# Gated linear attention: half of a head's first joint projection moved ahead of its first turn of keys, and low weight chunks moved ahead of the last chunk's gating

## The reference, cut to what matters

```python
q_g, k_g, v_g, r_g, gk_f, gk_b = ...              # columns of h @ w_in
lg_f = log_sigmoid(gk_f @ w_gk2_f + b_gk_f) / 16  # and lg_b
b = cumsum(logg, axis=3)                          # within a chunk
qe, ke, kd = q * exp(b), k * exp(-b), k * exp(b_last - b)
A = tril(qe @ ke.T);  o_intra = A @ v
kv_chunk = kd.T @ v
S_next = exp(b_last) * S + kv_chunk               # scan over chunks
o = o_intra + qe @ S
o_g = rms_norm(o_f + flip(o_b), g_gla) * silu(r_g)
```

## Time and profile before

| | us |
|---|---|
| median of 3 runs | 2572.76 |
| lowest and highest | 2570.7, 2573.95 |
| the profiled execution | 2568.94 |
| its span, first to last instruction | 2567.0 |
| PE busy in it | 2447.3 |
| DVE, ACT, POOL busy | 1816.8, 1403.8, 318.6 |

### The profile page before, as it was taken

The page is one execution under the profiler, slowest core; times in us unless marked ns, Lnnn a source line. Parts: engine busy times, 40 slices in busy tenths (PEclk is TensorE's granted clock), DMA queues, the critical chain, the costliest instruction groups (busy, mean ns, idle before and its releaser), DMA issues. The chain is left out here.

```text
span 2567.0 us, 38629 instructions
## 1 busy us (share of the span) xinstructions
PE 2447.3 (95%) x15139; PEld 1911.3 (74%) x15139; DVE 1816.8 (71%) x2810; ACT 1403.8 (55%) x2435; POOL 318.6 (12%) x312
## 2 busy tenths in 40 slices
PE   7999799999999999999999999996999999999996
PEld 4777799998887576666767887872677777777774
DVE  3767688886778446667587878557767777777676
ACT  4655577776454334344445543442666667666675
POOL 1333111110000001010101001000101201101013
PEclk9999899999999999999999999997999999999998
DMA  9410000000424101010003336546788988988889
GB/s 304 180 66 34 1 1 2 1 1 28 104 73 139 59 1 42 17 42 17 21 21 87 85 80 164 213 148 230 239 286 285 307 313 281 310 304 281 301 288 250
DMA packets 180376, 359.80 MB, mean 140 GB/s; under 512 B 9515, under 2 KB 41853, under 8 KB 178147
## 3 DMA queue, kind: packets, MB, share of 16 engines
q1 hardware_dynamic: 164220, 302.03, 33.3%
q0 software_dynamic: 14320, 54.53, 9.4%
q10 hardware_dynamic: 1654, 0.76, 0.1%
HBM read 302.25 MB, written 38.27 MB: 133 GB/s over the span
## 5 line engine op out<-in xcount | busy, mean ns | idle before, releaser
L3218 ACT ACTIVATE RWr<-R 128x1024 fp32r<-128x1024 f32 x384 | 377.8, 1053 | 68.4 <-PE ps L3103 64.0
L3350 DVE TENSOR_TENSOR W_low<-R,RWr 128x1024 fp32r<-128x1024 f32 x256 | 301.5, 1221 | 69.9 <-ACT RWr L3218 68.0
L3103 PE MATMUL ps<-RWr,R1r 128*128 128x512 f32 x1024 | 329.9, 396 | 4.5 <-DVE R1r L3337 2.3
L3103 PEld LDWEIGHTS ps<-RWr,R1r 128*128 128x128 f32 x1024 | 193.1, 189 | 57.7 <-issue 15.0
L1406 PE MATMUL ps<-W_high,tile_high 128*128 128x512 f32 x560 | 221.2, 395 | 9.0 <-DVE W_low L1511 6.1
L1406 PE MATMUL ps<-W_low,tile_high 128*128 128x512 f32 x560 | 220.0, 393 | 0.0
L1406 PE MATMUL ps<-W_high,tile_low 128*128 128x512 f32 x560 | 219.9, 393 | 0.0
L1854 PE MATMUL ps<-R3r 128*128 128x512 f32 (+1 forms) x640 | 188.6, 371 | 2.7 <-issue 2.7
L3350 DVE TENSOR_TENSOR tile_high<-R,RWr 128x1024 fp32r<-128x1024 f32 x128 | 150.9, 1221 | 37.7 <-ACT RWr L3218 37.3
L1440 ACT ACTIVATE tile_high<-R 128x512 fp32r<-128x512 f32 x140 | 87.6, 627 | 136.5 <-PE ps L1406 134.1
L3103 PE MATMUL ps<-RWr,R3r 128*128 128x512 f32 x480 | 156.2, 397 | 0.0
(11 more groups left out here) (463 smaller groups left out, 5448.0 us busy)
## 6 DMA issues: line engine op xcount, KB each, us to landing
R<-in_w_dram SPq DMA_DIRECT2D x96, 2048.0 KB, 13.0
RW<-RW POOLq DMA_DIRECT2D x16, 1024.0 KB, 7.0
RW<-in_w_in_dram SPq DMA_DIRECT2D x13, 1024.0 KB, 7.8
R<-in_w_mod_dram SPq DMA_DIRECT2D x6, 2048.0 KB, 9.5
RW<-in_w_in_dram SPq DMA_DIRECT2D x4, 2048.0 KB, 10.2
RW<-in_w_mod_dram SPq DMA_DIRECT2D x3, 2048.0 KB, 8.8
WK<-in_w_mod_dram SPq DMA_DIRECT2D x3, 2048.0 KB, 7.8
mix_scratch<-R SPq DMA_DIRECT2D x10, 512.0 KB, 3.1
```

The source lines that it names most:

```text
L3103: m = pe.matmul(bank(bank_of(e, i, j)), stat[a][:, k, :], w[b][:, k % 2, :], start=(k == 0 and z == 0), stop=(k == KD - 1 and z == 2))
L3218: act.activation(ring_high[n % RING], pair_raw[i][j][:, 2 * q:2 * q + 2, :], ACT.Copy).then_inc(S("weights_high"), 1)
L3350: dve.tensor_tensor(ring_low[n % RING], pair_raw[i][j][:, 2 * q:2 * q + 2, :], ring_high[n % RING].bitcast(F32), ALU.subtract).then_inc(S( ...
```

## The change

On PE, `joint` is given the halves that it is to run. In heads 1 to 3 the first half (`s = 0`, 12 matmuls) of joint projection 0 is issued directly behind `query_key(h, 2, 1)` and ahead of `turn_keys(h, 0)`; the second half stays in turn 1. On DVE, the low part of the first half tile and low weight chunks 4 to 7 are made ahead of `gated(h, 2)`; only the second half tile's low part stays behind turn 0's mask. Head 0, ACT, SP and GpSimd are as before.

```diff
-            def joint(h, n):
+            def joint(h, n, halves):
...
-                for s in range(2):
+                for s in halves:
                     pe.wait_ge(S("tile_split"), HALF_LOW + 2 * g + s + 1)
...
                 if j in r_step[h] and part < len(r_step[h][j]):
-                    joint(h, r_step[h][j][part])
+                    n = r_step[h][j][part]
+                    joint(h, n, (1,) if h and n == 0 else (0, 1))
...
                 if h == 0:
                     values(h, 0)
                     values(h, 1)
+                else:
+                    joint(h, 0, (0,))
                 for j in range(NI + 1):
...
-            def half_low(h, n):
+            def half_low(h, n, halves=(0, 1)):
                 t, g = r_order[n], h * NT + n
-                for s in range(2):
+                for s in halves:
...
                 gated(h, 1)
                 if h:
                     keep_finished(h - 1, TAIL[1])
+                    half_low(h, 0, (0,))
+                    for k in range(4, KD):
+                        joint_low(h, k)
                 gated(h, 2)
...
                     if h and j == 0:
-                        for k in range(4, KD):
-                            joint_low(h, k)
-                        half_low(h, 0)
+                        half_low(h, 0, (1,))
```

## The result

| | before | after |
|---|---|---|
| median, us (lowest to highest, runs) | 2572.86 (2570.7 to 2573.95, 4) | 2556.69 (2554.09 to 2559.33, 4) |
| ratio to before, 95% interval | | 0.9943 [0.9931, 0.9954] |
| profiled execution, us (span) | 2568.94 (2567.0) | 2559.33 (2557.5) |

Faster by 16.2 us by the medians and 14.7 by the ratio, 12 to 18 by the interval. A second set of runs of the same kernel, on another occasion, gave 2559.36 us against 2571.79, ratio 0.9947 [0.9933, 0.9960]: 12.4 us by the medians, 13.6 by the ratio. The forecast was 2560.6 us, a gain of 12.2.

What follows compares the result with a forecast made beforehand. PE, busy 95% of the span, was taken as the bound, idling in turn with DVE at head starts. Gains of 4.02, 5.65 and 2.80 us less 0.3 gave 12.2, so 2572.76 became 2560.6 us; range 2556.3 to 2567.3.

Steps and rivals of the forecast that it cites:

- Half the joint in the first gap: PE, starts of heads 1 and 2: half the joint, 2.77 us, fills the 1.89 us gap, pushing turn of keys 0.88.
- Low chunks ahead of the last gating: DVE, head starts: 3.06 us inserted, 2.50 of it formerly waiting; keys ready 0.5 us before PE wants them.
- Second half: Rest of the joint, head 2: DVE's last low half ready at 1187.0, PE arrives at 1187.2; second gap gone.
- rivals 3 and 5: 3: DVE takes the gap over, gain 3 to 6 us, chance 0.09; 5: late half projection delays PE, 2578.9, 0.04.
- Head 3: Start of head 3: half a joint is 1.48 us, so 0.42 us of the 1.90 us gap stays.
- The clock: Starts of heads 1 to 3: with the gaps gone, full clock returns, worth 1.56, 1.62 and 1.32, all 4.50 us.
- rival 2: Head starts: idle is regained but low clock stretches remain or recur elsewhere; gain 7.7 us, 2565.1 us, chance 0.22.
- the signs that the prediction names: Changed profile: key matmuls' end to first output product 9.1 us in heads 1 and 2, 6.9 in head 3.
- Cost of the split: Joint in heads 1 to 3: a second group start refills the array's pipe; 0.1 us a head, bounds 0 and 0.24.
- The sum: Heads 1 to 3 gain 4.02, 5.65 and 2.80, together 12.47 us, less 0.3 for splitting: 12.2 us.
- Reach to the end: Behind head 3: the merge's load follows its late turns, so PE's 3.33 us wait moves along and the gain survives.
- rival 4: Merge's load or a later stage absorbs the shift, or the half does not start before the keys: 2572 to 2573, chance 0.07.

Runs made afterwards that it cites:

- late_keys: The changed kernel with the first low half tile made three more times on DVE ahead of the last gating; ratio to before 0.9960.
- filler2: The kernel before with useless matmuls in its two gaps at the starts of heads 1 to 3 (4 and 4; 2 in head 3's second); ratio 0.9988.
- dve_alone: The kernel before with only DVE's part of the change, PE's order as before; ratio to before 0.9982.
- before_b: The kernel before, unchanged, in a second execution for its trace; head starts 20.59, 21.91 and 17.30 us.
- before_c: The kernel before, unchanged, in a third execution for its trace; head starts 20.42, 21.92 and 17.00 us.
- half_alone: The kernel before with PE's part and the one low half tile it needs; low chunks 4 to 7 stay behind the first mask; ratio to before 0.9978.
- half_filler2: half_alone with 4 useless matmuls (2 in head 3) in the gap ahead of the projection's second half; ratio to before 0.9982.

## Why the prediction was right, point by point

*Half the joint in the first gap.* Right. Expected 2.77 us, measured 2.97 (1178.92 to 1181.89). The turn of keys does not wait in heads 1 and 2.

*Low chunks ahead of the last gating.* Right, and to a tenth: keys 0.5 us before PE wants them, measured 0.58 (the last key product ends at 1180.89 + 0.42 = 1181.31, PE starts at 1181.89). DVE's instructions were no longer beside PE's half projection than alone (four chunks 2.49 us, 2.50 in rows 7). late_keys shows that beyond this cover the step would cost PE.

*Second half.* Right: no wait, so rivals 3 and 5 fall with it. *Head 3.* Right: 0.42 us of the gap expected to stay, 0.47 measured.

*The clock.* Full clock at all three starts was forecast and came. The sum had 8.0 us of idle (1.89 + 0.57, 1.89 + 2.14, 1.48) and 4.5 us of clock; the total was near, but the two terms are not independent, and what each is worth depends on which goes first. filler2 keeps the kernel before and its order and takes only the low clock away: 1.9 us, not 4.5. From there to after the order is worth 4.42, 4.44 and 2.74, 11.6 us, not 8.0. The reason is in heads 1 and 3, where the prediction read a second gap of 0.57 us and none. DVE decides when the joint starts: 5.79 us after the turn of keys in head 1 of before, 5.80 in head 2, 5.79 in head 1 of filler2. In head 1 the low clock had stretched PE's work into that time and so cost nothing; without it the gap is 2.1 us. In head 3 the same gap, which showed as none, is about 1.3 us from start to start (the joint starts 4.72 us after the turn in filler2, 3.42 in after; 5.79 against 3.42 is 2.4 us in head 1). The other way round, with the waits gone first, nothing hides a low stretch: in dve_alone head 1 takes 1.62 us more than head 2. So rival 2 ("idle returns, clock does not", 7.7 us) was priced by the right rule, and would by the head starts come to 13.5 less 4.5, 9.0 us; that is an estimate, as no run has the changed order with low stretches.

*A reading.* Head 3's 1.32 us of low clock compares two different lengths: 4.98 us runs to the joint's start, 3.66 to the modelled end of the intra products. From start to start it is 4.98 against 3.42, 1.56 us, as in head 1. And the signs that the prediction names, 9.1 and 6.9 us from the key matmuls' end to the first output product, do not fit its own sum, by which they would be 9.3 and 7.1; measured are 8.8 and 6.8 (15.88 and 13.89 less 7.07).

*Cost of the split.* 0.1 us a head was too little. The two halves take 2.97 and 2.84 us in head 2, 5.81 where the joint in one piece took 5.54: 0.27 us, just above the upper bound of 0.24.

*The sum.* 12.2 forecast, 13.5 in the head starts. The missing 1.3 us come from ends: a gap in the rows begins at the modelled end of the last matmul, but a following matmul can start before that (the joint at 1178.92, the keys' modelled end 1172.20 + 7.07 = 1179.27). In head 2 the joint comes 0.35 us earlier behind the keys than forecast, turns to second half take 3.35 us instead of 3.66, and the halves cost 0.17 more than the 0.1: 0.5 us, and head 1 is the same. In head 3, where DVE sets the turn of keys, only the stretch behind it is shorter than forecast: 0.3 us.

*Reach to the end.* The wait before the merge is still there and moved along: its first matmul comes 63.0 us behind head 3's first output product (62.9 before), so rival 4 falls.

```profile
1378.79 0.47 PE L1406 MATMUL ps<-W_high,tile_high 128*128 128x512 f32 x1 [3.45 <-DVE W_low L1511]
```

Behind head 3 the traces of the 13 executions in the table lie between 1239.8 and 1244.9 us with no order by kernel that I can show; 4.0 us lie between two traces of the kernel before alone (before_b and before_c), and single runs of one kernel in one set differ by 2 to 10.5 us. The 1.2 us (ratio) or 2.7 us (medians) by which the first set exceeds 13.5 are smaller than its interval; whether they are more than noise stays open.

The Trainium skill (TensorE: Matmul & The Clock Gate, section "What's actually happening") has the number of slow matmuls at a kernel's start vary from run to run; the prediction took that for every place in the kernel. For the start the traces agree: the first 50 us have a granted clock of 0.86 in one execution of the changed kernel and 0.76 in another. For places a millisecond in they do not show it: the head starts of three executions of the kernel before differ by at most 0.4 us in length and carry their low stretch each time.

## What to carry to other kernels

Where two engines wait for each other in turn (DVE idle while PE makes keys, PE idle while DVE gates them), move on each side a piece that needs nothing of the other: work for the idle engine, and the work it will ask for next. Do both; one alone gave 4 us each, both 13.5. Count idle time between starts, not from a modelled end. A low clock in front of a wait and the wait itself cover each other: book their sum, and before pricing one of them alone look whether the other stays.

## What the runs showed of the hardware

I had expected every gap of about 2 us to be followed by a low stretch. Of the gaps seen, those of 1.5 to 1.7 us (late_keys, three) and the 1.07 us in head 3 of half_alone had none, those of 1.9 to 2.1 us at one place had none (first gap of head 2, in before and in dve_alone) and elsewhere did, and with useless matmuls in the gaps the clock was 1.00 at every head start of four kernels. Whether size or instant decides is open. And 3.2 us won at the head starts need not arrive at the end: half_filler2 took 4.2 us longer behind them than half_alone, in one execution each, which is no more than two executions of one kernel can differ.
